# Moving 14 of GpSimd's pieces of weight sums from the combining stage to the attention

## The chip, the cores and the metric

The kernel runs on one core of one Trainium2 chip. The metric is device time in microseconds of one execution: median of 3 runs 2633.86 us (2628.06 to 2639.01).

## The reference, cut to what matters

One layer of a streaming encoder, in float32, for 2048 new frames and 64 frames that continue an older stream (2112 tokens in all):

```python
h = rms_norm(y, norm_attn)
qa, ka, va, qb, kb, vb = project_heads(h, pos, w_in, ...)      # one projection, QK-norm, rope on b
oa = band_attn_a_prompt(qa, ka, va, rel_bias_a)                # 8 heads, own chunk + 8 before
ob = window_attn_b_prompt(qb, kb, vb, sinks_b)                 # 8 heads on 2 kv heads, own chunk + 2 before
y = y + concat(oa, ob) @ w_out
gate, up = split(rms_norm(y, norm_ffn) @ w_gate_up, 2)         # 1024 x 5632
y = y + (silu(conv3(gate)) * up) @ w_down                      # 2816 x 1024
```

## The kernel before, in words

Four stages run one after the other, with a barrier of all engines between them: `project`, `attend`, `combine` (output projection and second norm) and `ffn`. Matrix products take each float32 operand as a rounded high part and a remainder, so that one product is three passes.

The FFN multiplies 2 x 2 blocks by Strassen's scheme with seven products. Three of them use the weights as they are; four use sums of weight blocks. These sums are prepared ahead of the FFN by GpSimd, in 132 **pieces** (`weight_pieces`): 88 for gate and up, then 44 for down. One piece (`WeightSums.piece`, lines 122 to 143) waits for its four 128 x 128 blocks, makes three subtractions (L129, L131, L133), rounds a high part (L135), subtracts for the low part (L137), issues the DMA that stores 512 KB in the scratch `t_gu` or `t_dn` (L142), and then, after a wait for the store that last used the buffer, issues the 256 KB load of the piece two further on (L117). There are three buffers. GpSimd runs its list strictly in order. The pieces are dealt to the first three stages by a table, `PREPARED`: 68, 42 and 22.

**Attention.** The queries are worked off in 17 tiles n of 128 (tile 0 is the 64 continuing frames). TensorE goes through 12 units u per tile: 8 heads of mixer A (up to 640 keys each), then 4 pairs of heads of mixer B. In a tile from the fifth on, an A unit begins with a small mask product (L909), a B unit with L904. Ahead of tile n the queries and keys must be split into high and low parts. ScalarE rounds: the keys of tile n+1 after unit 5 of tile n (L1009), the A queries of tile n+1 after unit 8 (L1015), the B queries of tile n after unit 3 (L1021). GpSimd subtracts: the keys (L855), the A queries (L860), the B queries (L866). TensorE's unit 0 of tile n waits for L860 of tile n, its unit 8 for L866 of tile n. GpSimd's order in tile n is

```python
split(n)            # L855, then weights(n, 0), then L860
weights(n, 1)
weights(n, 2)
split_b(n)          # L866
```

so that up to three places of a tile hold pieces: place 0 between L855 and L860, places 1 and 2 between L860 and L866. Which of the 43 places holds which pieces is worked out from the count:

```python
spots = [(n, j) for n in range(1, TILES + 1) for j in range(3) if j == 1 or n >= FULL]
spots += [(TILES + 1, j) for j in range(3)]
...
for at in range(first + (last - first) * spot // len(spots), first + (last - first) * (spot + 1) // len(spots)):
    prep.piece(at)
```

Tiles 1 to 4 have one place, tiles 5 to 16 three, and three places stand after the last tile. At the end GpSimd waits until all its stores have landed (`prep.stored`), ahead of the barrier. SyncE's load of the next keys and queries waits for L860, its load of the next B queries for L866.

**Combining.** Twelve steps (3 blocks of 704 tokens by 4 pairs of output rows). Each needs two weight loads of 512 KB (`w_raw`), a load of attention output (`o_raw`), one of x, and stores x1 and h2, all on SyncE's queue, in order. ScalarE rounds the loaded weights (L1389) and attention output (L1396), VectorE subtracts (L1445, L1451), TensorE multiplies (L81). GpSimd does nothing here but its pieces, one after the other.

Of the kernel before, what the change touches and what calls it, by code (L numbers as in the profile page):

```python
# [147 lines left out]
            self.nc.gpsimd.wait_ge(self.st[i], 16 * len(range(i, self.count, 3)))  # L148


PREPARED = ((0, 68), (68, 110), (110, 132))


def project(nc, x_tiles, x_rows, w_in, gains, gains_rope, rope_rows, ident, rel, q_a, k_a, qk_b, v_all, rel_rows,
# [2204 lines left out]
def encoder_step(nc, a):  # L2359
# [9 lines left out]
            scratch["q_a"], a["k_a"], a["qk_b"], a["v_all"], scratch["rel_rows"],  # L2369
            PREPARED[0], a["w_quads"], t_gu, t_dn)  # L2370
    attend(nc, scratch["q_a"], a["k_a"], a["qk_b"], a["v_all"], a["ka_cache"], a["kb_cache"], a["va_cache"],
           a["vb_cache"], scratch["rel_rows"], a["sinks"], a["ident"], scratch["oT"],
           PREPARED[1], a["w_quads"], t_gu, t_dn)
    combine(nc, scratch["oT"], a["xT"], a["w_o"], a["gains_ffn"], a["all_ones"], scratch["x1T"], scratch["h2T"],
            PREPARED[2], a["w_quads"], t_gu, t_dn)
    ffn(nc, scratch["h2T"], h_sums, scratch["x1T"], a["w_gu"], a["w_dn"], t_gu, t_dn, a["conv"], a["state"],
# [93 lines left out]
```

## Time and profile before

| | |
|---|---|
| median of 3 runs | 2633.86 us (2628.06 to 2639.01) |
| the profiled execution | 2626.59 us, span 2624.6 us |
| TensorE busy in the span | 2445.1 us, 93% |
| VectorE, ScalarE, GpSimd busy | 1729.6, 1164.2, 983.0 us |
| attention | from 474.6 us to about 961 us |
| combining | from about 961 us to about 1207 us |

Times in rows are microseconds from the span's start. A row of a timeline has the start, the duration, the engine and line, the operation, and in square brackets how long the engine sat idle before it and who released it. TensorE's clock is given as a share of full speed (2.4 GHz).

### The profile page before, as it was taken

The numbers are of one execution on the slowest core, as the hardware profiler recorded it, in microseconds if no ns is written. First come the engines' busy times: TensorE is split into PE (matmuls) and PEld (weight loads), VectorE is DVE, ScalarE is ACT, GpSimd is POOL, SyncE is SP. The second block draws the span as 40 slices with busy tenths as digits, with TensorE's granted clock in tenths as the row PEclk, the third lists the DMA queues.
The fourth block names the chain that finished last, engine by engine and source line by source line (L and its number), as shares of the span: only waits on it lengthen the run. The fifth ranks groups of instructions, "written<-read, shape, count | busy, mean of one in ns | idle before, by whom it ended". The sixth has DMA issues, their size and how long they took to land. (4 is left out here: it accounts for less than half of the span.)

```text
span 2624.6 us, 46088 instructions
## 1 busy us (share of the span) xinstructions
PE 2445.1 (93%) x15365; PEld 2329.9 (89%) x15365; DVE 1729.6 (66%) x3771; ACT 1164.2 (44%) x2650; POOL 983.0 (37%) x1134
## 2 busy tenths in 40 slices
PE   7999999589999969983999999999999999999998
PEld 4888888479999969883989999998999999999997
DVE  7666665556667655556666676767767677676766
ACT  5333332467766743222444343544444354443433
POOL 2888888357887778821030000113000011000001
PEclk9999999789999989996999999999999999999999
DMA  8676776647566659855677666787767678666665
GB/s 263 211 225 205 224 213 194 146 121 187 158 172 188 165 190 325 277 202 195 232 260 256 217 212 219 245 291 263 258 214 219 214 246 297 200 217 214 214 220 182
DMA packets 317707, 574.25 MB, mean 219 GB/s; under 512 B 35602, under 2 KB 166642, under 8 KB 317394
## 3 DMA queue, kind: packets, MB, share of 16 engines
q1 hardware_dynamic: 274402, 424.89, 51.5%
q0 software_dynamic: 38208, 142.80, 17.2%
q10 hardware_dynamic: 4912, 4.21, 0.5%
q8 instruction: 101, 1.65, 0.2%
q14 instruction: 84, 0.69, 0.1%
HBM read 442.72 MB, written 130.66 MB: 218 GB/s over the span
## 5 line engine op out<-in xcount | busy, mean ns | idle before, releaser
L2018 PE MATMUL ffn_z<-ffn_h_hi_S,ffn_w 128*128 128x352 f32 x1056 | 281.1, 329 | 17.7 <-DVE ffn_w L2147 11.5
L2018 PE MATMUL ffn_x<-ffn_h_hi_A,ffn_w 128*128 128x352 f32 x1056 | 269.1, 324 | 29.9 <-DVE ffn_h_lo_A L2142 29.0
L2018 PE MATMUL ffn_x<-ffn_h_hi_S,ffn_w 128*128 128x352 f32 x1056 | 276.8, 325 | 14.0 <-ACT ffn_sum L2046 12.4
L315 PE MATMUL project_z<-project_w_hi,project_h_hi 128*128 128x512 f32 (+3 forms) x680 | 255.5, 376 | 18.8 <-DVE project_w_lo L488 14.5
L1918 POOL TENSOR_TENSOR ffn_acc<-ffn_acc,ffn_sum 128x352 f32<-128x352 f32 x48 | 52.2, 1087 | 540.4 <-DVE ffn_sum L2264 482.4
L315 PE MATMUL project_z<-project_w_lo,project_h_hi 128*128 128x512 f32 (+3 forms) x680 | 252.1, 371 | 0.0
L315 PE MATMUL project_z<-project_w_hi,project_h_lo 128*128 128x512 f32 (+3 forms) x680 | 252.1, 371 | 0.0
L2147 DVE TENSOR_TENSOR ffn_w<-ffn_w_raw,ffn_w 128x512 fp32r<-128x512 f32 (+2 forms) x414 | 224.7, 550 | 11.4 <-ACT ffn_w L2096 11.2
L946 PE MATMUL attend_o<-attend_v,attend_prob_t 128*128 (+1 forms) x1680 | 224.9, 278 | 0.0
L1912 POOL DMA_DIRECT2D ffn_y_raw<-h_sums_scratch x2 | 1.1, 558 | 573.1 <-DVE ffn_y_lo_S L2169 573.1
L2018 PEld LDWEIGHTS ffn_x<-ffn_h_hi_A,ffn_w 128*128 128x128 f32 x1056 | 186.8, 189 | 31.5 <-DVE ffn_w L2147 28.9
L946 PEld LDWEIGHTS attend_o<-attend_v,attend_prob_t 128*128 128x128 f32 x1680 | 211.6, 194 | 0.6
L2018 PEld LDWEIGHTS ffn_z<-ffn_h_hi_S,ffn_w 128*128 128x128 f32 x1056 | 190.8, 192 | 23.2 <-DVE ffn_w L2147 23.1
L2096 ACT ACTIVATE ffn_w<-ffn_w_raw 128x512 fp32r<-128x512 f32 (+2 forms) x414 | 196.0, 500 | 22.5 <-issue 22.3
L2018 PEld LDWEIGHTS ffn_x<-ffn_h_hi_S,ffn_w 128*128 128x128 f32 x1056 | 188.0, 189 | 17.9 <-issue 17.8
L2018 PE MATMUL ffn_z<-ffn_h_lo_S,ffn_w 128*128 128x352 f32 x528 | 172.1, 326 | 0.0
L2018 PE MATMUL ffn_x<-ffn_h_lo_A,ffn_w 128*128 128x352 f32 x528 | 170.3, 322 | 0.0
L2018 PE MATMUL ffn_x<-ffn_h_lo_S,ffn_w 128*128 128x352 f32 x528 | 170.1, 322 | 0.0
L315 PEld LDWEIGHTS project_z<-project_w_hi,project_h_hi 128*128 128x128 f32 (+1 forms) x680 | 126.8, 186 | 46.5 <-DVE project_w_lo L488 11.3
L2018 PE MATMUL ffn_x<-ffn_y_hi_S,ffn_w 128*128 128x352 f32 x528 | 151.6, 325 | 8.7 <-DVE ffn_acc L2239 5.5
L2051 ACT ACTIVATE ffn_sum<-ffn_x 128x352 f32<-128x352 f32 x138 | 63.9, 463 | 213.9 <-PE ffn_x L2018 213.8
L81 PE MATMUL combine_z<-combine_o_hi,combine_w_hi 128*128 128x352 f32 x384 | 129.3, 337 | 30.6 <-DVE combine_w_lo L1445 20.4
(242 smaller groups left out, 6996.5 us busy)
## 6 DMA issues: line engine op xcount, KB each, us to landing
ffn_w<-t_gu_scratch SPq DMA_DIRECT2D x264, 512.0 KB, 4.0
ffn_w<-t_dn_scratch SPq DMA_DIRECT2D x240, 256.0 KB, 3.3
ffn_w_raw<-w_gu SPq DMA_DIRECT2D x198, 256.0 KB, 4.1
t_gu_scratch<-project_quads POOLq DMA_DIRECT2D x68, 512.0 KB, 4.5
ffn_w_raw<-w_dn SPq DMA_DIRECT2D x180, 128.0 KB, 3.5
project_quads<-w_quads POOLq DMA_DIRECT2D x68, 256.0 KB, 4.2
combine_w_raw<-w_o SPq DMA_DIRECT2D x24, 512.0 KB, 5.9
t_dn_scratch<-attend_quads POOLq DMA_DIRECT2D x22, 512.0 KB, 4.4
```

The source lines that it names most:

```text
L81: last = nc.tensor.matmul(out, w_parts[w](k), act_parts[a](k), start=(k == 0 and (w, a) == PASSES[0]), stop=(k == n_k - 1 and (w, a) == PA ...
L315: last = nc.tensor.matmul(z[c][0:w, 0:width], h[:, k, 0:w], ww[:, k, first:first + width], start=(k == 0 and h is hi and ww is w_hi), stop ...
L946: last = nc.tensor.matmul(o_ps[u % 2][:, head * P:(head + 1) * P], prob_t[u % 2][:, src:src + P], v[:, ds(tile + j, 1), pair * P:(pair + 1 ...
L1912: pool.dma_start(h_source(b, name), src).then_inc(h_ld[H_STAGE[name]], 16)
L1918: nc.gpsimd.tensor_tensor(total, total, part[:], ALU.add).then_inc(done, 1)
L2018: mm = nc.tensor.matmul(bank[:, 0:SUB], weights(c)[:, wp, k, :], (hi, lo)[a][name][:, 1 if short else k, :], start=first and k == 0 and (w ...
L2051: nc.scalar.activation(sum2[g % 2][:], x_ps[g % 2][:, 0:SUB], ACT.Copy).then_inc(sum2_ok, 1)
L2096: nc.scalar.activation(weights(c)[:, 0], raw(c), ACT.Copy)\
L2147: nc.vector.tensor_tensor(weights(c)[:, 1], raw(c), weights(c)[:, 0].bitcast(F32), ALU.subtract).then_inc(w_lo_ok, 1)
```

## The change

Only the table changes. The attention gets 56 pieces for its 43 places, the combining stage keeps 8. No arithmetic is added or left out.

```diff
-PREPARED = ((0, 68), (68, 110), (110, 132))
+PREPARED = ((0, 68), (68, 124), (124, 132))
```

By the formula above, 42 pieces on 43 places leave the first place (tile 1) empty and give one to each other. 56 pieces give at least one to each place and two to thirteen of them: place 1 of tile 4, place 2 of tiles 5 and 6, place 0 of tiles 8, 9 and 10, place 1 of tiles 11, 12 and 13, place 2 of tiles 14, 15 and 16, and the last place of all. Tile 7 keeps three pieces.

GpSimd's row in tile 9 before, from the key split (L855) to the split of the A queries (L860); `attend_quads` are the buffers of the pieces:

```order
L855 TENSOR_TENSOR attend_keys<-attend_raw,attend_keys 64x10x128
L129 TENSOR_TENSOR attend_quads0<-attend_quads0 128x256
L131 TENSOR_TENSOR attend_quads0<-attend_quads0 128x128
L133 TENSOR_TENSOR attend_quads0<-attend_quads0 128x128
L135 CAST attend_quads0<-attend_quads0 128x512
L137 TENSOR_TENSOR attend_quads0<-attend_quads0 128x512
L142 DMA t_gu_scratch<-attend_quads0 256x4x128
L117 DMA attend_quads2<-w_quads 128x512
L860 TENSOR_TENSOR attend_q_lo<-attend_raw,attend_q_hi 128x1024
```

and after the change, the end of what stands between the same two instructions (L855 stands six rows ahead of the first row shown):

```order
L142 DMA t_dn1_scratch<-attend_quads0 256x4x128
L117 DMA attend_quads2<-w_quads 128x512
L129 TENSOR_TENSOR attend_quads1<-attend_quads1 128x256
L131 TENSOR_TENSOR attend_quads1<-attend_quads1 128x128
L133 TENSOR_TENSOR attend_quads1<-attend_quads1 128x128
L135 CAST attend_quads1<-attend_quads1 128x512
L137 TENSOR_TENSOR attend_quads1<-attend_quads1 128x512
L142 DMA t_dn1_scratch<-attend_quads1 256x4x128
L117 DMA attend_quads0<-w_quads 128x512
L860 TENSOR_TENSOR attend_q_lo<-attend_raw,attend_q_hi 128x1024
```

One piece stood between the two, and two stand there now; L860 comes after both.

GpSimd's row at the beginning of the attention before: the loads of the first two pieces, L866 of tile 0, then L855, L860 and L866 of tile 1 and L855 and L860 of tile 2:

```order
L117 DMA attend_quads0<-w_quads 128x512
L117 DMA attend_quads1<-w_quads 128x512
L866 TENSOR_TENSOR attend_q_lo<-attend_raw_b,attend_q_hi 128x1024
L855 TENSOR_TENSOR attend_keys<-attend_raw,attend_keys 64x10x128
L860 TENSOR_TENSOR attend_q_lo<-attend_raw,attend_q_hi 128x1024
L866 TENSOR_TENSOR attend_q_lo<-attend_raw_b,attend_q_hi 128x1024
L855 TENSOR_TENSOR attend_keys<-attend_raw,attend_keys 64x10x128
L860 TENSOR_TENSOR attend_q_lo<-attend_raw,attend_q_hi 128x1024
```

and after the change, from L855 of tile 1 to L855 of tile 2:

```order
L855 TENSOR_TENSOR attend_keys<-attend_raw,attend_keys 64x10x128
L860 TENSOR_TENSOR attend_q_lo<-attend_raw,attend_q_hi 128x1024
L129 TENSOR_TENSOR attend_quads0<-attend_quads0 128x256
L131 TENSOR_TENSOR attend_quads0<-attend_quads0 128x128
L133 TENSOR_TENSOR attend_quads0<-attend_quads0 128x128
L135 CAST attend_quads0<-attend_quads0 128x512
L137 TENSOR_TENSOR attend_quads0<-attend_quads0 128x512
L142 DMA t_gu_scratch<-attend_quads0 256x4x128
L117 DMA attend_quads2<-w_quads 128x512
L866 TENSOR_TENSOR attend_q_lo<-attend_raw_b,attend_q_hi 128x1024
L855 TENSOR_TENSOR attend_keys<-attend_raw,attend_keys 64x10x128
```

Tile 1 had no piece and has one, behind L860 and ahead of L866. The other pieces behind L860 are added in the same manner: in tiles 5, 6 and 11 to 16 there are 14 rows between L860 and L866 before and 21 now (two pieces, three pieces), and behind the last L866 there are three pieces before and four now. In the combining stage GpSimd's row is cut off after its eighth piece.

## Rows read from the trace of the kernel before

**Rows 1.** Stretches of the program: busy us of each engine, clock, DMA share, GB/s.

```profile
core 0: us, PE busy (x) PEld busy (x) DVE busy (x) ACT busy (x) POOL busy (x), PEclk, DMA share, GB/s
600.00:950.00 350.00, 348.02 (x2955) 339.51 (x2955) 240.08 (x665) 245.43 (x581) 284.75 (x303) 1.00 0.62 167
1020.00:1090.00 70.00, 70.00 (x438) 69.58 (x437) 39.42 (x44) 22.14 (x27) 60.84 (x70) 1.00 0.85 283
1090.00:1140.00 50.00, 36.31 (x202) 34.20 (x201) 28.49 (x31) 12.70 (x15) 32.29 (x36) 0.93 0.86 307
1140.00:1196.00 56.00, 49.91 (x296) 48.52 (x294) 27.82 (x37) 14.24 (x17) 0.00 (x0) 0.94 0.39 136
```

**Rows 2.** Groups of GpSimd instructions: busy us, mean ns, idle before them, releaser.

```profile
L855 POOL TENSOR_TENSOR attend_keys<-attend_raw,attend_keys 64x1280 fp32r<-64x1280 f32 x16 | 46.5, 2904 | 49.7 <-ACT attend_keys L1009 49.7
L866 POOL TENSOR_TENSOR attend_q_lo<-attend_raw_b,attend_q_hi 128x1024 fp32r<-128x1024 f32 x17 | 40.3, 2368 | 36.6 <-ACT attend_q_hi L1021 36.5
L860 POOL TENSOR_TENSOR attend_q_lo<-attend_raw,attend_q_hi 128x1024 fp32r<-128x1024 f32 x16 | 38.2, 2385 | 10.7 <-ACT attend_q_hi L1015 10.7
L117 POOL DMA_DIRECT2D attend_quads<-w_quads x42 | 23.3, 556 | 10.3 <-DVE attend_keys L1201 10.2
```

**Rows 3.** Timeline, GpSimd, one tile of the attention (start, duration, idle before).

```profile
start us, us, engine line op out<-in xcount [idle before <-releaser]
864.50 2.41 POOL L860 TENSOR_TENSOR attend_q_lo<-attend_raw,attend_q_hi 128x1024 fp32r<-128x1024 f32 x1
866.82 0.77 POOL L129 TENSOR_TENSOR attend_quads<-attend_quads 128x256 f32<-128x256 f32 x1
...
872.58 0.76 POOL L129 TENSOR_TENSOR attend_quads<-attend_quads 128x256 f32<-128x256 f32 x1
...
878.74 2.36 POOL L866 TENSOR_TENSOR attend_q_lo<-attend_raw_b,attend_q_hi 128x1024 fp32r<-128x1024 f32 x1 [0.42 <-ACT attend_q_hi L1021]
884.10 2.91 POOL L855 TENSOR_TENSOR attend_keys<-attend_raw,attend_keys 64x1280 fp32r<-64x1280 f32 x1 [3.01 <-ACT attend_keys L1009]
887.09 0.73 POOL L129 TENSOR_TENSOR attend_quads<-attend_quads 128x256 f32<-128x256 f32 x1
...
892.79 2.41 POOL L860 TENSOR_TENSOR attend_q_lo<-attend_raw,attend_q_hi 128x1024 fp32r<-128x1024 f32 x1
```

**Rows 4.** Timeline, TensorE, the same tile: first A unit, first B unit, next tile.

```profile
867.60 0.19 PE L909 MATMUL attend_s<-attend_mask_k,attend_mask_q 128*128 128x64 bf16 x1
...
886.54 0.27 PE L904 MATMUL attend_s<-attend_mask_k,attend_mask_q 128*128 128x257 bf16 x1
...
895.90 0.19 PE L909 MATMUL attend_s<-attend_mask_k,attend_mask_q 128*128 128x64 bf16 x1
```

**Rows 5.** Waits of TensorE from 595 to 955 us (total, times, longest).

```profile
PE attend_s L909 <- POOL attend_q_lo L860: 0.6, 1, 0.6
```

**Rows 6.** Timeline, TensorE, the place of that wait.

```profile
612.38 0.20 PE L909 MATMUL attend_s<-attend_mask_k,attend_mask_q 128*128 128x64 bf16 x1 [0.64 <-POOL attend_q_lo L860]
```

**Rows 7.** Timeline, GpSimd, tiles 1, 4 and 5.

```profile
522.70 2.35 POOL L866 TENSOR_TENSOR attend_q_lo<-attend_raw_b,attend_q_hi 128x1024 fp32r<-128x1024 f32 x1 [8.82 <-ACT attend_q_hi L1021]
...
596.28 2.36 POOL L866 TENSOR_TENSOR attend_q_lo<-attend_raw_b,attend_q_hi 128x1024 fp32r<-128x1024 f32 x1 [6.41 <-ACT attend_q_hi L1021]
...
623.73 2.40 POOL L866 TENSOR_TENSOR attend_q_lo<-attend_raw_b,attend_q_hi 128x1024 fp32r<-128x1024 f32 x1
629.08 2.92 POOL L855 TENSOR_TENSOR attend_keys<-attend_raw,attend_keys 64x1280 fp32r<-64x1280 f32 x1 [2.95 <-ACT attend_keys L1009]
```

**Rows 8.** Timeline, GpSimd and SyncE, end of the attention.

```profile
952.92 1.04 POOL L142 DMA_DIRECT2D t_dn_scratch<-attend_quads  x1 [0.30 <-POOL attend_quads L137]
961.91 0.55 POOL L117 DMA_DIRECT2D combine_quads<-w_quads  x1 [7.96 <-POOLq L61]
...
953.58 4.81 SPq L788 DMA_DIRECT2D oT_scratch<-attend_o_t  x2
```

**Rows 9.** DMA issues of the page: KB each, median us from issue to landing.

```profile
t_dn_scratch<-attend_quads POOLq DMA_DIRECT2D x22, 512.0 KB, 4.4
```

**Rows 10.** Timeline, TensorE, in the combining stage and in the FFN after a wait.

```profile
1105.04 0.66 PE L81 MATMUL combine_z<-combine_o_hi,combine_w_hi 128*128 128x352 f32 x1 [4.33 <-DVE combine_w_lo L1445]
1105.49 0.49 PE L81 MATMUL combine_z<-combine_o_lo,combine_w_hi 128*128 128x352 f32 x1
1105.79 0.49 PE L81 MATMUL combine_z<-combine_o_hi,combine_w_lo 128*128 128x352 f32 x1
...
1110.42 0.32 PE L81 MATMUL combine_z<-combine_o_hi,combine_w_hi 128*128 128x352 f32 x1
1110.58 0.32 PE L81 MATMUL combine_z<-combine_o_lo,combine_w_hi 128*128 128x352 f32 x1
...
1817.66 0.43 PE L2018 MATMUL ffn_z<-ffn_h_hi_S,ffn_w 128*128 128x352 f32 x1 [2.51 <-DVE ffn_w L2147]
```

**Rows 11.** Waits of TensorE from 1085 to 1145 us.

```profile
PE combine_z L81 <- DVE combine_w_lo L1445: 7.6, 4, 4.3
PE combine_ms L1366 <- DVE combine_ssq L1468: 3.3, 1, 3.3
PE combine_z L81 <- DVE combine_o_lo L1451: 2.8, 2, 1.7
```

**Rows 12.** Timeline, ScalarE, the longest wait for a weight load.

```profile
1090.35 1.06 ACT L1389 ACTIVATE combine_w_hi<-combine_w_raw 128x1024 fp32r<-128x1024 f32 x1 [12.47 <-DMA combine_w_raw<-w_o]
```

**Rows 13.** VectorE groups from 1020 to 1131 us, with GpSimd at work.

```profile
L1468 DVE TENSOR_TENSOR combine_ssq<-combine_ssq,combine_x_sq 128x704 f32<-128x704 f32 x11 | 12.8, 1165 | 0.2
```

**Rows 14.** The same group from 1140 to 1196 us, without GpSimd.

```profile
L1468 DVE TENSOR_TENSOR combine_ssq<-combine_ssq,combine_x_sq 128x704 f32<-128x704 f32 x7 | 6.2, 888 | 0.2 <-ACT combine_x_sq L1410 0.2
```

## The prediction

> **What bounds the kernel now.** The stretches come first [rows 1]. In the attention, from 600 to 950 us, TensorE is busy 348.02 of 350 us at full clock: it is the bound there. GpSimd is busy 284.75 of the same 350 us. In the combining stage TensorE is busy 70.00 of 70 us from 1020 to 1090, but only 36.31 of 50 from 1090 to 1140. So a gain in combining can come only from the gaps of about 1090 to 1150, and a loss in the attention comes from anything that holds TensorE there.
>
> By the sum, GpSimd has room in the attention: its waits of the four groups add up to 49.7 + 36.6 + 10.7 + 10.3 = 107 us [rows 2], and 14 pieces are less than that. The sum misleads, since the room isn't where the pieces go. The timeline of one late tile shows it [rows 3]. From L860 to the next L860 are 28.29 us. In them GpSimd is idle 0.42 us ahead of L866 and 3.01 ahead of L855, 3.43 in all; the other 24.86 are work. A piece is 5.76 us long: two follow each other at 866.82 and 872.58, the first of them starting where L860 ends. TensorE's rows of the same tile [rows 4] put its unit 0 at 867.60 and the next at 895.90: 28.30 us, the same period. L860 ends at 866.91 and at 895.20 (start and duration); TensorE starts 0.7 us after it.
>
> Is that 0.7 us slack, or does TensorE wait? In one tile it did wait: 0.6 us for L860 [rows 5], at 612.38 [rows 6], where L860 had ended 0.1 us before. In that tile the delay from L860 to TensorE is therefore 0.1 us, and in the other tiles some 0.6 us are slack. These 0.6 us are all that lies between the present order and a TensorE that waits for GpSimd.
>
> **The change part by part.** TensorE, VectorE, ScalarE and SyncE keep their instructions and their order. Only GpSimd's row changes, and each moved piece brings five computations, one store of 512 KB and one load of 256 KB with it. It is also moved past GpSimd's own later splits, for which TensorE, and SyncE's next loads, wait.
>
> *Tiles 8, 9, 10: two pieces ahead of L860.* L855 can't start before ScalarE has rounded the keys (after unit 5 of TensorE's tile), so this place can't use GpSimd's idle time. L860 comes 5.76 us later, less the 0.6 of slack: TensorE waits 5.2 us at the head of the tile. It happens anew in each, because ScalarE's rounding, and with it L855, has moved along with TensorE. 3 x 5.2 = 15.5 us (5.16 each).
>
> *The clock in these waits.* After a wait of 4.33 us in the combining stage TensorE begins a matmul every 0.30 us (1105.49, 1105.79), and from 1110.42 on every 0.16; after a wait of 2.51 us it shows 0.43 us for the first and no slow run [rows 10]. So the low level (1.2 GHz) lasted from 1105.04 to about 1110.2, 5.1 us, in which at the full clock (2.4 GHz) the same work takes about 2.7: 2.4 us lost. TensorE being the bound up to unit 5, this is added to each of the three waits: 7.2 us. Waits of 2.3 us and less, below, I take as free of it; if they weren't, the loss would be hidden, since there GpSimd is the bound (28.3 + 2.4 = 30.7 us of TensorE beside 30.6 of GpSimd).
>
> *Tiles 5, 6 and 11 to 15: a third piece between L860 and L866.* Here the idle 3.43 us are used up first, then GpSimd is busy all the time, and the tile takes 24.86 + 5.76 = 30.62 us, 2.33 more than 28.29. Tile 5 had no wait ahead of L866 and 2.95 ahead of L855 [rows 7], so it costs the next tile 5.76 - 2.95 - 0.6 = 2.2; tile 6 costs 2.3; tile 11 has the whole 3.43 and the slack again: 5.76 - 3.43 - 0.6 = 1.7; tiles 12 to 15 cost 2.33 each, 9.3. Together 15.5 us. Part of each wait will show at unit 8 (L866 now ends some 19.6 us after L860, TensorE gets to unit 8 after 886.54 - 867.60 = 18.94), the rest at unit 0.
>
> *Tiles 1 and 4.* The extra piece stands ahead of an L866 that waits 8.82 us in tile 1 and 6.41 in tile 4 for ScalarE [rows 7]. Both are above 5.76: hidden. If that cover were gone they would cost up to 5.8 each.
>
> *The end of the attention.* Behind L860 of tile 16 stand two more pieces than before, 11.5 us, and L860 has lost its 0.6 us of lead: GpSimd ends 12.1 us later in relation to TensorE. Before, its last store was issued at 952.92 and lands after some 4.4 us [rows 9], at 957.3; the other chain, TensorE's last output and SyncE's store, is issued until 953.58 + 4.81 = 958.4, and the next stage starts at 961.91 [rows 8]. GpSimd's slack is thus between 1.1 us (958.4) and 4.6 (961.91). I take 3.2, nearer the start of the next stage, since SyncE's store has to land too. Cost 8.9 us, bounds 7.5 and 11.0.
>
> *Combining.* GpSimd started at 961.91 and worked until about 1131 on 22 pieces, 7.7 us each, so eight end near 1023. The 14 others moved 14 x 768 KB = 10.8 MB in some 108 us, 100 GB/s of the 283 to 307 that all moved [rows 1]. From 1020 to 1090 nothing is to be had. From 1090 to 1140 TensorE is idle 13.7 us and loses 2.4 to the low clock as above. The waits there are 7.6 us for rounded weights, 2.8 for attention output and 3.3 for the sum of squares [rows 11]. The first two go back to loads: ScalarE waited 12.47 us for one [rows 12]. VectorE is also slower beside GpSimd: the same sum takes 1165 ns with it and 888 without [rows 13, 14]. At most the stage gives back 13.7 + 2.4, and 3.0 more for the clock of 0.94 after 1140 (6% of 49.91), 19 us; at least nothing, if SyncE's own transfers make the gaps. I take the waits for weights and output and the clock, 7.6 + 2.8 + 2.4 = 12.8, less a little, 12 us.
>
> The Trainium skill (SBUF — State Buffer, "Who interferes with whom") says that a VectorE instruction with two inputs in SBUF and a GpSimd instruction that reads SBUF exclude each other for a whole instruction, and that DMA never contends with a compute engine. The slower sum of squares agrees with the first half. If only that lock held the stage back, the gain would be at most 31 VectorE instructions of 1090 to 1140 by 0.28 us, 8.6 us, and the forecast some 3 us higher. The rest of the sum doesn't use it.
>
> Sum: 15.5 + 7.2 + 15.5 + 8.9 - 12 = +35 us. Against the profiled execution's 2626.6 us that is 2662. The median of the runs shown, 2633.9, is 7.3 above it; the forecast for a median is 2669 us.
>
> **The rivals.** *GpSimd's room takes it all, combining gains: faster.* The 107 us of idle GpSimd would have to be usable, that is, TensorE would have to have more lead on L860 than 0.6 us, for instance if pieces shortened when GpSimd never stops. For it speaks the sum of idle time, against it the wait of 0.6 us in tile 5. It decides from 5.2 us of lead. Then only -12 is left: 2622. Chance 0.05.
>
> *The gaps in combining stay.* SyncE's own loads come in bursts in one queue, and each step needs about 3 MB of them. The attention loses its 47 us and nothing comes back: 2681. For it speaks the wait of 3.3 us that is not for a load; against it that the gaps lie just where GpSimd still worked. Chance 0.14.
>
> *The cheaper attention.* The clock stays up after waits of 5 us (the one of 4.33 was followed by the low level, which speaks against it), and the last store is hidden behind the barrier's own work. 15.5 + 15.5 - 12 = +19: 2653. Chance 0.11.
>
> **How the numbers follow.** The forecast has the remaining 0.70. Its own parts range from 15.5 + 15.5 + 7.5 - 19 = +20 (no clock, full gain) to 47 + 2 = +49 (a later last store, no gain). That is 2654 to 2683 on the median of 2634; the three runs of before differ from it by up to 6 us, so the lower end is put at 2645 and the upper at 2686. What a measurement of this kernel can tell from no change is about 0.5%, 13 us: 2621 to 2647. All cases but the first lie above, the cheaper attention only by 6 us. Slower 0.91, the same 0.05, faster 0.04.
>
> **What would show it.** In the attention TensorE's waits should name GpSimd: about 5 us ahead of L909 in three tiles running, each followed by some 5 us at the low clock; then about 2 us per tile in seven others, split between L909 and L904; none in tiles 2 to 5. GpSimd's waits ahead of L855 and L866 should be gone in tiles 12 to 16. The tile's period should read 28.3, about 30.6 and about 36 us. Combining should begin some 47 us later, and from there last 12 us less, with VectorE's sum near 888 ns after the eighth piece. The forecast is wrong if the tiles 8 to 10 still take 28.3 us, or if combining shortens by more than 19 us.

## The result, and the profile after

| | before | after |
|---|---|---|
| median (runs) | 2631.89 us (4; 2628.06 to 2639.01) | 2670.96 us (4; 2667.30 to 2674.77) |
| ratio after / before | | 1.0145, 95% interval 1.0115 to 1.0175 |
| profiled execution, span | 2626.59, 2624.6 us | 2674.77, 2672.9 us |
| TensorE busy | 2445.1 us | 2459.3 us |

The changed kernel is 38 us slower (30 to 46 by the interval). The forecast was +35 us, 2669 us. It stood on the median of 2633.86 us of three runs of the kernel before; with the fourth run that median is 2631.89.

The windows of the kernel after come first (columns as in [rows 1]). Combining now begins at 1015 us, so its window lies 50 us later than that of before.

```profile
600.00:950.00 350.00, 320.79 (x2633) 309.61 (x2632) 215.82 (x597) 221.07 (x520) 298.50 (x331) 0.98 0.66 178
1140.00:1190.00 50.00, 43.84 (x256) 41.46 (x255) 24.94 (x32) 13.39 (x16) 0.00 (x0) 0.97 0.75 263
```

In the same 350 us of the attention TensorE is busy 321 us where it was 348. In the combining stage the stretch with the gaps has 43.84 of 50 us instead of 36.31. The attention lost more than combining gained. Who is waited for is in the table of TensorE's waits in the attention (total, times, longest), first of before, from 500 to 975 us, where the only wait for GpSimd is that of [rows 5]:

```profile
PE attend_t L930 <- ACT attend_prob_t L1047: 19.3, 22, 3.7
```

and of after, from 500 to 1030 us:

```profile
PE attend_s L909 <- POOL attend_q_lo L860: 26.5, 11, 5.0
PE attend_t L930 <- ACT attend_prob_t L1047: 22.8, 21, 5.4
...
PE attend_s L904 <- POOL attend_q_lo L866: 3.3, 8, 0.8
```

The one wait of 0.6 us for GpSimd has become 19 waits, 29.8 us in all. A second thing stands there that the forecast had not: the longest wait for ScalarE went from 3.7 to 5.4 us.

The waits for L860 one by one, from TensorE's timeline of after, answer to [rows 6]. Of the 11, those at 617.01, 783.52, 844.33, 875.02, 937.03 and 967.74 are left out:

```profile
647.78 0.20 PE L909 MATMUL attend_s<-attend_mask_k,attend_mask_q 128*128 128x64 bf16 x1 [1.70 <-POOL attend_q_lo L860]
...
679.12 0.20 PE L909 MATMUL attend_s<-attend_mask_k,attend_mask_q 128*128 128x64 bf16 x1 [2.25 <-POOL attend_q_lo L860]
...
712.69 0.23 PE L909 MATMUL attend_s<-attend_mask_k,attend_mask_q 128*128 128x64 bf16 x1 [4.96 <-POOL attend_q_lo L860]
...
747.85 0.23 PE L909 MATMUL attend_s<-attend_mask_k,attend_mask_q 128*128 128x64 bf16 x1 [4.01 <-POOL attend_q_lo L860]
...
906.32 0.20 PE L909 MATMUL attend_s<-attend_mask_k,attend_mask_q 128*128 128x64 bf16 x1 [1.60 <-POOL attend_q_lo L860]
```

These are tiles 6 and 7, then 8 and 9 with 4 to 5 us each (10 follows below), then 14. Tile 11 starts at 813.37 without a wait, since no extra piece stands ahead of its L860. The wait of tile 10 and some of the first matmuls of its units 0 and 1 show the clock, as [rows 10] did:

```profile
783.52 0.23 PE L909 MATMUL attend_s<-attend_mask_k,attend_mask_q 128*128 128x64 bf16 x1 [4.95 <-POOL attend_q_lo L860]
...
784.09 0.47 PE L913 MATMUL attend_s<-attend_keys,attend_q_lo 128*128 x1
784.36 0.47 PE L913 MATMUL attend_s<-attend_keys,attend_q_hi 128*128 x1
...
787.19 0.19 PE L909 MATMUL attend_s<-attend_mask_k,attend_mask_q 128*128 128x64 bf16 x1
...
787.45 0.31 PE L913 MATMUL attend_s<-attend_keys,attend_q_lo 128*128 x1
...
789.32 0.19 PE L909 MATMUL attend_s<-attend_mask_k,attend_mask_q 128*128 128x64 bf16 x1
```

Behind the wait a matmul of L913 takes 0.47 us and begins 0.27 behind the one before (1.2 GHz), at 787.45 it takes 0.31 (2.4 GHz). Unit 0 takes 3.67 us where unit 1 takes 2.13.

GpSimd's own row in tile 9 of after answers to [rows 3]: between the two L860, at 745.37 and 781.03, lie 35.66 us.

```profile
745.37 2.35 POOL L860 TENSOR_TENSOR attend_q_lo<-attend_raw,attend_q_hi 128x1024 fp32r<-128x1024 f32 x1
...
761.25 2.37 POOL L866 TENSOR_TENSOR attend_q_lo<-attend_raw_b,attend_q_hi 128x1024 fp32r<-128x1024 f32 x1 [3.10 <-ACT attend_q_hi L1021]
766.62 2.91 POOL L855 TENSOR_TENSOR attend_keys<-attend_raw,attend_keys 64x1280 fp32r<-64x1280 f32 x1 [3.00 <-ACT attend_keys L1009]
...
781.03 2.36 POOL L860 TENSOR_TENSOR attend_q_lo<-attend_raw,attend_q_hi 128x1024 fp32r<-128x1024 f32 x1
```

GpSimd is idle 3.10 and 3.00 us in this tile, in which TensorE waited 4 to 5 us for it at either end: its idle time and the demand for it lie at different places.

Times from one L860 to the next in us, summed from GpSimd's timelines:

| tiles | before | after | difference | forecast |
|---|---|---|---|---|
| 1 to 2 | 20.97 | 24.15 | +3.2 | 0 |
| 2 to 5 | 77.45 | 77.88 | +0.4 | 0 |
| 5 to 7 | 56.15 | 62.05 | +5.9 | 4.5, and 0.6 of used lead |
| 7 to 11 | 112.75 | 133.65 | +20.9 | 22.7, less 0.6 of lead won back |
| 11 to 16 | 142.25 | 154.96 | +12.7 | 11.0, and 0.6 of used lead |

### The profile page after: what moved, and what is told of

It reads as the page before. It is cut to its first block and busy times, and to the rows that moved or that the text cites. A ratio compares the mean times of both kernels' runs of the same rounds, so it can differ in the third digit from the quotient of the medians.

```text
span 2672.9 us, 46088 instructions
## 1 busy us (share of the span) xinstructions
PE 2459.3 (92%) x15365; PEld 2339.1 (88%) x15365; DVE 1718.9 (64%) x3771; ACT 1165.6 (44%) x2650; POOL 969.9 (36%) x1134
## 5 line engine op out<-in xcount | busy, mean ns | idle before, releaser
L2147 DVE TENSOR_TENSOR ffn_w<-ffn_w_raw,ffn_w 128x512 fp32r<-128x512 f32 (+2 forms) x414 | 226.4, 555 | 11.6 <-ACT ffn_w L2096 11.4
L2056 ACT ACTIVATE ffn_sum<-ffn_x 128x352 f32<-128x352 f32 x138 | 64.2, 465 | 217.2 <-PE ffn_x L2018 214.7
L2051 ACT ACTIVATE ffn_sum<-ffn_x 128x352 f32<-128x352 f32 x138 | 64.0, 464 | 213.4 <-PE ffn_x L2018 213.2
```

The lines of the kernel that those rows point to most:

```text
L2051: nc.scalar.activation(sum2[g % 2][:], x_ps[g % 2][:, 0:SUB], ACT.Copy).then_inc(sum2_ok, 1)
L2056: nc.scalar.activation(sum3[g % 2][:], x_ps[g % 2][:, 0:SUB], ACT.Copy).then_inc(sum3_ok, 1)
L2147: nc.vector.tensor_tensor(weights(c)[:, 1], raw(c), weights(c)[:, 0].bitcast(F32), ALU.subtract).then_inc(w_lo_ok, 1)
```

## The experiments

A difference in us is here the recorded ratio of the runs, times the median of before. The ratio is not the quotient of the two medians, and the plain difference of the medians lies up to 4 us from it. Where a kernel has a single run, the two times are given and no ratio.

In kernels with a table of pieces (below) the lines from about 840 on stand one or two later: L861 is L860 of before, L910 is L909, L867 is L866.

### The combining stage alone

```diff
-PREPARED = ((0, 68), (68, 110), (110, 132))
+PREPARED = ((0, 68), (68, 110), (110, 118))
...
-    ffn(..., t_gu, t_dn, a["conv"], ...)
+    ffn(..., t_gu, t_dn[:4] + [t_dn[3], t_dn[3]], a["conv"], ...)
```

The last 14 pieces are computed nowhere; the FFN reads earlier sums in their place, as many bytes as before.

> The attention keeps its 42 pieces, combining does only the first 8 of its 22; the other 14 are left out and the FFN reads other, finished sums in their place, so the result is not the reference's. Theory 'late gaps' (combining gains only where TensorE had gaps, after 1090 us, by loads that land sooner and a faster VectorE): 10 to 12 us less than before, no change ahead of 1085 us, the waits for the weight remainder (7.6 us) gone. Rival 'own bursts' (SyncE's loads make the gaps by themselves): less than 3 us.

Measured: 2617.54 us against 2632.72, ratio 0.9948 (0.9931 to 0.9965), -13.7 us. TensorE's idle time in this kernel's stretch of 1085 to 1135 us (timeline) answers to [rows 11]:

```profile
1093.73 0.42 PE L81 MATMUL combine_z<-combine_o_hi,combine_w_hi 128*128 128x352 f32 x1 [0.69 <-DVE combine_w_lo L1445]
1102.31 0.43 PE L81 MATMUL combine_z<-combine_o_hi,combine_w_hi 128*128 128x352 f32 x1 [0.68 <-DVE combine_w_lo L1445]
1110.48 0.43 PE L81 MATMUL combine_z<-combine_o_hi,combine_w_hi 128*128 128x352 f32 x1 [0.23 <-DVE combine_w_lo L1445]
```

The waits for weights are down from 7.6 to 1.6 us, those for attention output are gone. The wait for the sum of squares has grown from 3.3 to 4.7. What went away on the way there is seen in the issues of SyncE's loads from 1060 to 1130 us (KB each, median us to landing), in the kernel before:

```profile
combine_w_raw<-w_o SPq DMA_DIRECT2D x7, 512.0 KB, 8.4
combine_o_raw<-oT_scratch SPq DMA_DIRECT2D x3, 704.0 KB, 10.6
```

and with eight pieces:

```profile
combine_w_raw<-w_o SPq DMA_DIRECT2D x8, 512.0 KB, 7.0
combine_o_raw<-oT_scratch SPq DMA_DIRECT2D x3, 704.0 KB, 8.4
```

Each load lands 1.4 to 2.2 us sooner. ScalarE's longest wait for a weight load [rows 12] is still 11.69 us. So SyncE's own transfers make most of that wait, as the rival "the gaps in combining stay" said.

TensorE's longest wait, the one of 4.33 us at 1105.04 [rows 10], ended with VectorE and not with a load. The weights had landed and were rounded by 1098.56 (ScalarE's L1389). VectorE's timeline of before shows that from L1451 on it worked without a pause until it came to L1445:

```profile
1092.59 1.81 DVE L1468 TENSOR_TENSOR combine_ssq<-combine_ssq,combine_x_sq 128x704 f32<-128x704 f32 x2
1096.27 2.18 DVE L1451 TENSOR_TENSOR combine_o_lo<-combine_o_raw,combine_o_hi 128x704 fp32r<-128x704 f32 x2 [1.87 <-ACT combine_o_hi L1396]
1098.37 4.61 DVE L1486 SCALAR_TENSOR_TENSOR combine_h<-combine_x,combine_g_x,combine_n_c 128x704 f32<-128x704 f32 x3
...
1103.77 1.21 DVE L1445 TENSOR_TENSOR combine_w_lo<-combine_w_raw,combine_w_hi 128x1024 fp32r<-128x1024 f32 x1
```

and with eight pieces:

```profile
1095.97 1.69 DVE L1451 TENSOR_TENSOR combine_o_lo<-combine_o_raw,combine_o_hi 128x704 fp32r<-128x704 f32 x2 [0.65 <-ACT combine_o_hi L1396]
1097.59 2.67 DVE L1486 SCALAR_TENSOR_TENSOR combine_h<-combine_x,combine_g_x,combine_n_c 128x704 f32<-128x704 f32 x3
...
1101.04 1.22 DVE L1445 TENSOR_TENSOR combine_w_lo<-combine_w_raw,combine_w_hi 128x1024 fp32r<-128x1024 f32 x1
```

From the start of L1451 to the start of L1445 VectorE takes 7.50 us beside GpSimd and 5.07 without it. These 2.4 us are two thirds of the 3.65 by which the wait became shorter (4.33 to 0.68). Another 0.3 come from L1451, which starts sooner, its load having landed sooner, and 0.9 from TensorE, which gets there later.

In the profiled execution the stage is 8.2 us shorter (249.68 us from SyncE's first transfer to the FFN's first matmul, 257.85 before). The rest of the 13.8 us between the two profiled executions lies in the FFN (5.3 us). The FFN takes 1400 to 1410 us in the twelve profiles of this document, and this one is the shortest; so the 5.3 us are not shown to come from the pieces.

How much of this needs all 14 pieces to be away? In the next kernel 16 stay in combining, and six (of which no sum is computed; the FFN reads earlier ones) are left out.

```diff
-PREPARED = ((0, 68), (68, 110), (110, 132))
+PREPARED = ((0, 68), (68, 110), (110, 126))
...
+    ffn(..., t_gu, t_dn[:5] + [t_dn[4]], a["conv"], ...)
```

> As the one before, but combining does the first 16 pieces and leaves out the last 6 (the FFN reads others; not the reference's result). Theory 'late gaps': the last six pieces are the ones that run beside the gaps, so nearly the whole gain is there already, 8 to 11 us. Rival 'by volume' (each piece less gives the same): 6/14 of what 14 pieces give, some 4 us.

Measured: 2621.94 us, ratio 0.9961 (0.9948 to 0.9974), -10.3 us. By these ratios the six last pieces carry three quarters of the gain, but the two intervals overlap widely, and the rival (six of 14 pieces give 6/14 of the gain, 5.9 us) isn't excluded by them alone. The profiles speak against it: the stage takes 250.92 us here, 6.9 less than before, of the 8.2 with eight pieces. These six pieces are those that lie beside the gaps of 1090 to 1131 us.

### The attention alone

```diff
-PREPARED = ((0, 68), (68, 110), (110, 132))
+PREPARED = ((0, 68), (68, 124), (110, 132))
```

14 pieces are computed twice, first in the attention, then again in combining.

> The attention does 56 pieces as in the changed kernel, combining still does all 22 (14 of them a second time). Theory 'lead' (TensorE is held wherever GpSimd's query split comes over 0.6 us late): some 48 to 51 us more than before, all of it ahead of combining. If the two stages are independent, this and the run with 8 pieces in combining alone add up to the change. Rival 'pieces cost in combining' (half of the loss of the attention is a price of fewer idle cycles later): well under 45 us.

Measured: 2681.35 us against 2632.72, ratio 1.0185 (1.0168 to 1.0202), +48.7 us. With the kernel of eight pieces, 48.7 - 13.7 = +35.0 us, inside the interval of the whole change (30 to 46). The two parts add up within what these runs can tell, some 6 us. In the profiled execution, itself 7 us above the kernel's median, tiles 1 to 16 take 45.7 us more than before (43.1 in after). Its combining stage, with the same 22 pieces as before, takes 263.40 us, 5.5 more than before. Whether that comes from the attention or from this one execution is open.

### The place of the extra pieces in tiles 8, 9 and 10

Here the number of pieces at each place is a table:

```diff
-            spots = [(n, j) for n in range(1, TILES + 1) for j in range(3) if j == 1 or n >= FULL]
-            spots += [(TILES + 1, j) for j in range(3)]
+            given = {(n, j): 1 for n in range(2, TILES + 1) for j in range(3) if j == 1 or n >= FULL}
+            given |= {(TILES + 1, j): 1 for j in range(3)}
+            given |= {(1, 1): 1, ..., (8, 2): 2, (9, 2): 2, (10, 2): 2}
...
+                for _ in range(given.get((n, j), 0)):
+                    prep.piece(next(following))
```

All is as after, but the second piece of tiles 8, 9 and 10 stands behind L860 (place 2) instead of ahead of it (place 0).

> The changed kernel, but the extra piece of tiles 8, 9 and 10 stands behind the split of the A queries (L860, place 2) and not ahead of it. The count of pieces and their transfers stay. Theory 'lead': these tiles then take 30.6 us and not 33.6 to 35.7, no wait of 5 us and no low clock in them: 13 to 15 us less than the changed kernel, +24 on the kernel before. Rival 'volume' (the price of a piece in the attention is its transfers and its use of memory ports, wherever it stands): the same as the changed kernel, +38.

Measured: 2654.01 us against 2632.72, ratio 1.0096 (1.0077 to 1.0114), +25 us, 13 less than the change by the two ratios. TensorE's waits from 500 to 1030 us in this kernel:

```profile
PE attend_s L910 <- POOL attend_q_lo L861: 16.3, 11, 2.2
PE attend_s L905 <- POOL attend_q_lo L867: 4.5, 10, 1.0
```

No wait for GpSimd is over 2.2 us, and the windows show the clock, first in after (700 to 800 us), where the three tiles lie:

```profile
700.00:800.00 100.00, 85.85 (x672) 83.52 (x671) 54.71 (x150) 56.04 (x134) 78.12 (x91) 0.91 0.60 166
```

then in this kernel (690 to 790 us):

```profile
690.00:790.00 100.00, 96.11 (x810) 92.95 (x809) 66.02 (x185) 68.49 (x160) 87.37 (x96) 1.00 0.67 184
```

TensorE is busy 10 us more in the same 100. From L861 of tile 7 to that of tile 11 it takes 119.82 us, 7.1 more than before (112.75), where after takes 20.9 more. Three pieces moved past one instruction are worth 13.8 us in the trace.

### One piece, ahead of L860 or behind it

The same at its smallest: the kernel before with 43 pieces in the attention (and 21 in combining), the one more in tile 9, at place 0 or at place 2.

```diff
+            given |= {(9, 0): 2}
```

> The kernel before with one piece more in the attention (43) and one less in combining (21): a second piece ahead of the split of the A queries (L860) in tile 9. Theory 'lead': the distance from L860 of tile 8 to L860 of tile 9 grows by 5.8 us, TensorE waits 5.2 us, drops to the low clock, and from L860 of tile 8 to that of tile 11 there are 7.6 us more than before. Rival 'volume': under 2.5 us more, and the same as for the next kernel.

```diff
+            given |= {(9, 2): 2}
```

> The same, but the second piece stands in tile 9 behind L860 (place 2). Theory 'lead': GpSimd's idle 3.4 us and the lead of 0.6 us take most of it; TensorE waits 1.7 us, no low clock, and from L860 of tile 8 to that of tile 11 there are 1.7 us more than before. Rival 'volume': the same as for the kernel before this one.

One run each on the same chip: 2635.55 us (ahead) and 2631.50 (behind), against 2628.69. From L861 of tile 8 to that of tile 11: 91.43 us ahead, 87.04 behind, 84.45 before. So the price is +7.0 ahead (7.6 by the forecast's terms) and +2.6 behind (1.7). The wait of the first kernel, from TensorE's timeline:

```profile
732.86 0.23 PE L910 MATMUL attend_s<-attend_mask_k,attend_mask_q 128*128 128x64 bf16 x1 [4.96 <-POOL attend_q_lo L861]
```

and those of the second:

```profile
745.91 0.28 PE L905 MATMUL attend_s<-attend_mask_k,attend_mask_q 128*128 128x257 bf16 x1 [0.45 <-POOL attend_q_lo L867]
...
757.15 0.20 PE L910 MATMUL attend_s<-attend_mask_k,attend_mask_q 128*128 128x64 bf16 x1 [1.61 <-POOL attend_q_lo L861]
```

In both GpSimd has the same 5.76 us more to do. Ahead of L860, 7.0 - 4.96 = 2.0 us come on top of the wait; the window of 720 to 740 us has a mean clock of 0.83 there, and 1.00 in the other kernel. In the second kernel the two waits add up to 2.06 us of its 2.6, so 0.5 come on top. Nothing else in the two kernels differs, so the 2.0 us go with the long wait; the clock and the filling up again behind the wait are not shown apart.

### Tile 1

In tile 1 ScalarE's wait for the values (timelines, kernel before, then after) is what changed:

```profile
526.15 0.28 ACT L1047 ACTIVATE attend_prob_t<-attend_t 128x128 f32<-128x128 f32 x1 [2.11 <-DMA attend_v<-v_all]
```

```profile
530.34 0.28 ACT L1047 ACTIVATE attend_prob_t<-attend_t 128x128 f32<-128x128 f32 x1 [5.29 <-DMA attend_v<-v_all]
```

The extra piece is moved from tile 1 to tile 3, all else being as after:

```diff
+            given |= {(4, 1): 2, ..., (17, 2): 2, (3, 1): 2}
```

> The changed kernel, with the piece of tile 1 moved to tile 3 (which gets two). In the changed kernel tile 1 took 3.2 us longer though GpSimd had room. Theory 'shared transfers' (the store and load of the piece, 768 KB, are under way at the time of the loads of the next keys and values, which ScalarE waits for): from L860 of tile 1 to that of tile 2 21 us again and not 24.2, and in tile 3, where the loads have more time, under 1.5 us are added. Rival 'GpSimd late' (its splits come late in tile 1): then tile 3, with two pieces and less room (5.4 us of idle time for 5.8), would pay the same 3 us.

Measured: 2669.20 us in one run (2628.69 before), which can't tell 3 us. The trace can: from L861 of tile 1 to that of tile 2 it takes 21.34 us again (24.15 after, 20.97 before), and the wait is 2.47. In all profiles of this document tile 1 takes 20.97 to 21.99 us where it is empty (nine) and 24.15 to 25.35 where it has the piece (three). Tile 3, with its second piece, takes 24.76 us (24.45 before): it doesn't pay, as the rival "GpSimd late" would have it. Tile 2 takes 26.53 us here instead of 24.89 to 25.10, with no piece added in it. In the kernels whose tiles 1 and 2 are as before it takes 23.8 to 26.8, so the trace doesn't tell whether some of the 2.8 us come back there.

What holds the values up is in the issues of 517 to 531 us. Before:

```profile
attend_raw<-k_a SPq DMA_DIRECT2D x2, 256.0 KB, 5.0
attend_v<-v_all SPq DMA_DIRECT2D x1, 320.0 KB, 4.9
attend_raw<-qk_b SPq DMA_DIRECT2D x2, 64.0 KB, 4.7
```

After:

```profile
t_gu_scratch<-attend_quads POOLq DMA_DIRECT2D x1, 512.0 KB, 5.6
attend_raw<-k_a SPq DMA_DIRECT2D x2, 256.0 KB, 7.2
attend_v<-v_all SPq DMA_DIRECT2D x1, 320.0 KB, 7.0
attend_quads<-w_quads POOLq DMA_DIRECT2D x1, 256.0 KB, 8.3
attend_raw<-qk_b SPq DMA_DIRECT2D x2, 64.0 KB, 6.6
```

The same 14 us carry 3.07 MB instead of 2.31, the difference being the piece's 768 KB, and these loads of SyncE land some 2 us later. With tile 1 empty they are back at 5.0, 5.2 and 4.8 us. GpSimd itself was in time: its L866 at 523.72 still waited 3.15 us for ScalarE.

The Trainium skill (DMA: Bandwidth & Descriptors, "Issuing engines are not separate DMA queues") says that transfers run on the same 16 DMA engines and interleave whoever starts them. The landing times here agree: the same 320 KB take 7.0 us instead of 4.9.

### One more piece at the very end

```diff
+            given |= {(17, 2): 2}
```

(43 pieces in the attention, 21 in combining.)

> The kernel before with one piece more in the last place of the attention (43) and one less in combining (21). Theory 'slack of the last store': in the changed kernel the end of the attention came 10.0 us later for 12.1 us more of GpSimd's work, so the slack is 2.1 us, and one piece more (5.8 us) costs 3.7 us from L860 of tile 16 to the first transfer of combining. Rival 'hidden by the barrier': under 1 us.

Measured: 2636.68 us in one run, against 2628.69. From the last L860 to SyncE's first transfer of combining it takes 43.74 us, 40.34 before: +3.4. GpSimd's last store is issued 37.58 us behind that L860 (962.02), 31.83 before (952.92), so the piece brings 5.75 us, and 2.4 of them were covered. The rival "hidden by the barrier" (under 1 us) is out. The other 4.6 us of the difference between the two runs lie elsewhere: tile 2 alone took 1.9 us more in the profile, with nothing changed in it.

### A version that uses only the early tiles

Extra pieces only where GpSimd waits over 4 us ahead of L866 and TensorE does not wait for it, behind L860 of tiles 2, 3 and 4. First with one more in tile 0, behind L866:

```diff
+PREPARED = ((0, 68), (68, 114), (114, 132))
...
+            given |= {(0, 0): 1, (2, 1): 2, (3, 1): 2, (4, 1): 2}
...
             split_b(0)
+            weights(0, 0)
```

> A version meant to beat both: four pieces more than before in the attention (46) and 18 in combining. The extra ones stand where GpSimd is idle by the trace: one behind the B queries' split of tile 0, one each in tiles 2, 3 and 4; tile 1 stays empty. Theory 'lead': no wait of TensorE for GpSimd, under 3 us more in the attention, and combining, whose last pieces run beside TensorE's gaps, gives back some 7 of the 10 us that leaving out six gave: 3 to 6 us less than before (0.998). Rival 'volume': 4 x 3.4 us more in the attention (48 us by 14 pieces), 7 back: 6 us more.

Measured: 2627.99 us against 2630.57, ratio 0.9989 (0.9976 to 1.0003): no change that can be told.

```diff
+PREPARED = ((0, 68), (68, 113), (113, 132))
...
+            given |= {(2, 1): 2, (3, 1): 2, (4, 1): 2}
```

> As the one before, without the piece in tile 0 (45 pieces, 19 in combining). Theory 'lead': under 2 us more in the attention, 4 to 6 back in combining: 2 to 4 us less than before. Rival 'volume': 3 x 3.4 more, 5 back: 5 us more.

Measured: 2625.55 us against 2630.57, ratio 0.9982 (0.9970 to 0.9995): 5 us faster than before (1 to 8), and some 43 us faster than the change by the two ratios. The attention costs next to nothing for its three pieces: from L861 of tile 1 to that of tile 16 it takes 410.0 us (409.6 before), and from there to combining 40.35 (40.34 before). TensorE's waits of 1020 to 1145 us in this kernel:

```profile
PE combine_z L81 <- DVE combine_w_lo L1446: 5.4, 2, 4.3
PE combine_ms L1367 <- DVE combine_ssq L1469: 4.8, 1, 4.8
```

The waits for attention output are down to 0.9 us, those for weights only from 7.6 to 5.4. Combining is 0.8 us shorter in the profile (257.07 us), so it shows some 0.4 us of gain up to the FFN, and the five us of the medians are not traced to the pieces.

The kernel with one piece more away isn't faster, and the two intervals overlap. Its profile has combining 3.5 us shorter (254.34 us), but the attention 1.8 us longer (488.63 us from SyncE's first transfer of the attention to that of combining, 486.82 before). TensorE's longest wait for ScalarE in tile 0 is 5.0 us there and 3.5 to 3.8 in the eleven other profiles. So by this one profile tile 0 is not a free place either.

## Why the prediction was right

It was right in sign, in size and, in the attention, in the mechanism. In combining it was right about the gain but put it down to the wrong cause in part. Its steps, with what each was and what it turned out to be:

- **Two pieces ahead of L860** (15.5 us) and **the clock in these waits** (7.2 us): 20.9 us from tile 7 to 11. The waits are 4.96, 4.01 and 4.95 us, 13.9 in all. Between their starts lie 35.16, 35.67 and 29.85 us (tile 11 starts at 813.37); without the waits inside them these are 31.15, 30.72 and 29.85, over 28.30 by 2.9, 2.4 and 1.6, 6.8 us for the clock and the refilling. The forecast had 22.7, less the lead of 0.6 won back. The wait of 4.01 instead of 5.2 is the one behind the longest of these. Single pieces ahead and behind show the step alone, 7.0 and 2.6 us; moving the three behind L860 gives back 13.8.
- **A third piece between L860 and L866** (15.5 us): the periods are 30.69, 31.30, 30.71 and 30.71 us for tiles 12 to 15, 30.62 foreseen. Tiles 5 and 6 took 5.9 us more and tiles 11 to 15 took 12.7 more, where 5.1 and 11.6 were foreseen. The split of the waits is as told, 1.6 us at unit 0 and 0.2 to 0.8 at unit 8. These waits were taken as free of the low clock. They were, but not in every kernel: in that with tile 1 empty the wait of 1.71 us at 646.66 was followed by 4 us at 0.57. It cost nothing, as the forecast had said of such a case: the period is 31.38 us, 31.36 in after.
- **Tiles 1 and 4 hidden**: right for tile 4 (28.30 us from 4 to 5, 28.11 before), wrong for tile 1, +3.2 us. The step counted the piece's time on GpSimd, which was covered, but not its 768 KB, although it had said itself that every moved piece brings them. SyncE's loads of the next tile are under way just then. ScalarE already waited 2.11 us there for one of them before. The empty tile 1 took the wait back to 2.47 us. Such a wait doesn't say by itself that there is no room: ScalarE waits 2.47 us for the values in tile 2 of before as well, and with one piece more there it waits 2.73.
- **The end of the attention** (8.9 us): from TensorE's start of tile 16 to SyncE's first transfer of combining, 37.24 us before, 47.27 after: +10.0. GpSimd's last store and first issue in combining, timeline of after, answer to [rows 8]:

```profile
1008.48 1.03 POOL L142 DMA_DIRECT2D t_dn_scratch<-attend_quads  x1 [0.30 <-POOL attend_quads L137]
1015.49 1.10 POOL L117 DMA_DIRECT2D combine_quads<-w_quads  x2 [5.98 <-POOLq L61]
```

  and SyncE's first of combining:

```profile
1015.01 0.39 SPq L1290 DMA_DIRECT2D combine_o_raw<-oT_scratch  x1
```

  It comes 6.5 us behind the last store's issue (1008.48), where before it was 8.5 (952.92 to 961.43). So GpSimd's slack was 2.0 us, not 3.2. The experiment with one piece gives 2.4. The forecast chose 3.2 between 1.1 and 4.6, too far from the lower end.
- **Combining** (-12 us): from SyncE's first transfer to the FFN's first matmul 257.85 us before (961.43 to 1219.28), 247.89 after (1015.01 to 1262.90): -10.0. All that is left of the gaps from 1070 to 1190 us are two rows:

```profile
1146.96 0.42 PE L81 MATMUL combine_z<-combine_o_hi,combine_w_hi 128*128 128x352 f32 x1 [1.49 <-DVE combine_w_lo L1445]
...
1183.39 2.71 PE L1366 MATMUL combine_ms<-combine_ssq,combine_ones 128*128 128x352 f32 x4 [4.62 <-DVE combine_ssq L1468]
```

  Of the 12.8 us forecast 1.5 stay for weights, and the wait for the sum of squares, left out of the gain, has grown from 3.3 to 4.6: 12.8 - 1.5 - 1.3 = 10.0. That fits by the numbers alone, since it takes the 2.4 us of the clock as won in full. VectorE's sum of squares is back at 888 ns, as told:

```profile
L1468 DVE TENSOR_TENSOR combine_ssq<-combine_ssq,combine_x_sq 128x704 f32<-128x704 f32 x11 | 9.8, 888 | 0.2
```

  and with eight pieces the loads land 1.4 to 2.2 us sooner. The step that fails is "the first two go back to loads": the largest of these waits, 4.33 of the 7.6 us, stood behind a slow VectorE, and 2.4 of the 3.65 us that went from it are VectorE's. No run took away the transfers and left GpSimd's computations, or the other way round, so how the whole gain divides is not shown.

  The rule of the Trainium skill (SBUF — State Buffer, "Who interferes with whom") that the prediction weighed, a lock between VectorE and GpSimd, would have given at most 8.6 us by the forecast's estimate; the stage gave 10.0. VectorE's slow instructions agree with the lock, with the 2.4 us at the largest wait as its clearest share; the sooner loads are no part of it.

Measured in the traces, the steps come to 39.4 us up to TensorE's start of tile 16 without tile 1 (forecast 38.2), 3.2 for tile 1, 10.0 and -10.0, together +42.6. The medians differ by 39. Stages that the change doesn't touch differ by 1.0 us (project) and 4.7 (FFN) between the two profiled executions, so the 3.6 between 42.6 and 39 are within what two executions differ by. All four misses of size went the same way, against the change, and the middle value of 35 was low by them, by 7.6 us. That the forecast of 2669 us lies within 2 us of the median is therefore in part luck: the medians differ by less than the profiled executions, and the base of the forecast was 2 us above the later median.

**The rivals.** "GpSimd's room takes it all" is out: 19 waits name GpSimd, though it is still idle 33.4 us ahead of L855 and 26.1 ahead of L866 in the attention after the change ([rows 2] had 49.7 and 36.6). "The gaps in combining stay" is out by the kernel with eight pieces, -13.7 us, though it has something to it: ScalarE's longest wait for weights and the wait for the sum of squares stayed. (A step moves 3.8 MB by SyncE's issues, two of 512 KB and four times 704 KB, not about 3 as the forecast says.) "The cheaper attention" is out on both of its legs: the clock fell in all three waits, and the last store was not hidden.

## What to carry to other kernels

Before moving work into an engine's idle time, look where in its order the idle time stands and what is queued behind the moved work: the same piece cost 7.0 us ahead of the instruction that the busiest engine waits for, 2.6 behind it, and next to nothing in tiles 2 to 4, where GpSimd waited over 4 us behind it. Count the moved work's transfers as well as its instructions, and look at what else is being loaded at that moment: in tile 1 the same piece cost 3.2 us that way. In a stage whose gaps lie at its end it may be enough to take away what runs beside them: six of 14 pieces gave most of the gain, by their ratios three quarters. Before a wait is put down to a load, look whether the engine in between was idle or merely slow.

## What the runs showed of the hardware

- The waits of TensorE of 4.0 to 5.0 us in the attention were followed by the low clock (0.50 in the 4 us behind 712.69 and behind 747.85, 0.62 in 783.5 to 788). A wait of about 5 us cost some 2 us beside itself. Behind waits of 1.6 to 2.25 us it stayed at 1.00, both in after (640 to 700 and 840 to 940 us) and in the kernel whose waits for GpSimd are all 2.2 us or less. But the length of a wait alone doesn't settle it: the clock was 0.57 in the 4 us behind the wait of 1.71 at 646.66 in the kernel with tile 1 empty. In the combining stage of the kernel with one piece behind L860 it was 0.58 behind a wait of 2.37 us (1098.90) and 0.65 behind one of 2.94 (1111.29).
- A store of 512 KB and a load of 256 KB from GpSimd held up SyncE's loads of keys and values by about 2 us each, small ones as much as large ones (4.7 to 6.6 us for 64 KB, 4.9 to 7.0 for 320 KB), and those of the B queries by 1.5 (4.0 to 5.5 for 256 KB).
- GpSimd's computations slow VectorE, its transfers don't show. In the kernel before, from 1020 to 1200 us, the 14 sums of 128x704 (L1468) that met no computation of GpSimd took 883 to 893 ns each, and the six that met one took 1396 ns as a mean, up to 1982. The mean of 1165 ns [rows 13] is a mixture of both kinds. The two sums at 1092.59 took 1.81 us, 0.88 and 0.89 each: GpSimd was then waiting for its own store, which was under way (until 1093.67). L1486 is 947 ns against 1427, L1451 882 against 1318. GpSimd is slowed as well: its L137 takes 1.27 to 1.28 us in the attention and up to 2.16 in combining.
